# A two-layer decoder trunk on one Trainium2 core: one chunk of expert weights is brought into partitions 0 to 63 alone

## The chip, the cores and the metric

The kernel runs on one core of one Trainium2 chip. The metric is the device time of one execution in microseconds (us). Three executions of the kernel before took 1298.48, 1296.72 and 1298.28 us: a median of 1298.28.

## The reference

Input is one sequence of 256 tokens of 1024 numbers, all in float32. Layer 0 is attention (eight block-sparse heads, eight indexer-sparse heads) and a dense SwiGLU of 2816. Layer 1 is multi-head latent attention and then the part that this case is about, a mixture of eight experts of which each token uses two:

```python
top_val, top_idx = lax.top_k(logits, TOP_K)          # 2 of 8
gates = jax.nn.softmax(top_val, axis=-1)
combine = jnp.sum(jax.nn.one_hot(top_idx, N_EXPERTS) * gates[..., None], axis=1)
y = jnp.zeros_like(ht)
for e in range(N_EXPERTS):
    y = y + combine[:, e:e + 1] * swiglu(ht, w_gate[e], w_up[e], w_down[e])
```

`w_gate_o` and `w_up_o` are 1024 x 3584 for each expert, `w_down_o` is 3584 x 1024. Every expert has some tokens, so all 24 matrices are read: 352 MB out of the 424 MB that the kernel moves.

## The kernel before, in words

The first 400 us are layer 0 and the attention of layer 1. They read their weights in chunks of up to 1 MB through a ring `raw`.

The experts are computed in four pairs (`PAIRS`), a "large" expert with up to 96 tokens (three tiles of 32) and a "small" one with up to 64 (two tiles of 32). Tokens beyond that go through spare rounds, which don't run on this input. The weights of a pair come in 48 chunks (`PAIR_CHUNKS`), each of 128 partitions x 3584 numbers, 14,336 bytes in each partition and 1792 KB in all. A pair has six phases of eight chunks: large gate, large up, small gate, small up, large down, small down (`PHASES`, L59). Chunk k of gate or up holds rows 128 (k % 8) to 128 (k % 8) + 127 of the matrix, one row in each partition.

The whole stage is a ring of eleven places (`RING`, L270; `E_PLACES`): chunk n goes to place n % 11 and raises that place's own semaphore by 16 when it has landed. SyncE (SP) issues one transfer for each chunk, in order (`expert_chunk`, L388). Before chunk n it waits until TensorE has finished chunk n - 11 (`mm_done`, L392). A down row of 1024 numbers does not divide 3584, so two down chunks are used together, and `before` says which one frees the place. The last chunk of all comes in two transfers (L401, L402). So the order of work is written out by hand: SP's program is one list of transfers, TensorE's is one list of products, and the two are tied by `mm_done` in one direction and by the landing semaphores in the other.

TensorE packs four products side by side in its columns: a tile of 32 tokens is the stationary operand for one quarter of the output columns, and four such quarters are accumulated at once. For one gate or up chunk of the small expert that is 2 tiles x 2 column pieces (512 and 384) x 4 quarters = 16 matmul instructions in the program, which the profile counts as 32 (`tile_products`, L2292). Between the chunks TensorE also turns picks and results (L2235, L2342), brings back results (L2244), and gathers the next pair's tokens (`gather`, L2221) into PSUM. From there ScalarE and VectorE copy them to `xe` (L812, L1564).

In the last pair, chunk k = 23 (`SG + 7`) is the eighth and last chunk of the small gate. It is number 167 of the 192 chunks. In `pair` TensorE reaches it just after `turn_picks`.

Of the kernel before, what the change touches and what calls it, by code (L numbers as in the profile page):

```python
# [18 lines left out]
P = 128  # L19
S = 256  # L20
TT = S // P
D = 1024
DC = D // P
# [26 lines left out]
NT = 512  # L50
# [7 lines left out]
HALF = P // 2  # L58
# [6 lines left out]
E_PLACES = 11  # L65
# [5 lines left out]
X_CAP = L_CAP + S_CAP  # L71
YC = D // 4
SPARES = NE + PAIRS

SPARE_DOWN = 4 * FE_TILES
SPARE_CHUNKS = SPARE_DOWN + FFE // P // 2
# [6 lines left out]
def hybrid_trunk(nc, x, rel_bias, mix_norm_e, w_in_e, moba_q_norm, moba_k_norm, dsa_q_norm,  # L83
# [30 lines left out]
    C_OUTO = plan([rows(w_out_o, kh * 512, 4, n * NT, NT) for n in range(2) for kh in range(2)])  # L114
    C_ROUTE = plan([rows(w_router, 0, DC, 0, NE)])
    C_MOE = len(chunks)

    with ExitStack() as ctx:
        sems = {}

        def sem(name):
            if name not in sems:
                sems[name] = ctx.enter_context(nc.semaphore(name))
            return sems[name]
# [108 lines left out]
        xT, z1 = place(z + 2 * EW, "xT", [P, DC, S])  # L233
        ffg, _ = place(z1, "ffg", [P, D])
        junk, _ = place(z2, "junk", [P, TT, NT])
        xe = nc.alloc_sbuf_tensor_at("xe", [P, DC, X_CAP], f32, offset=a_hi_at)
        back_l = nc.alloc_sbuf_tensor_at("back_l", [P, L_TILES, S], f32, offset=a_hi_at + 4 * DC * X_CAP)
        xpick = cst[:, K_MASK:K_MASK + TT * X_CAP].rearrange("p (t s) -> p t s", t=TT)
# [40 lines left out]
        def place_of(n):  # L279
            return RING[n % E_PLACES]  # L280

        def landed(n):
            return ex_full[n % E_PLACES], 16 * (n // E_PLACES + 1)

        def before(n):

            m = n - E_PLACES
            return m + 1 if m % PAIR_CHUNKS >= DOWN and m % 2 == 0 else m

        LAST = PAIRS * PAIR_CHUNKS - 1  # L290
        LAST_AT = NT + D

# [45 lines left out]

            return [u for u in range(FE_TILES) if done(u) + late + u % 2 == k]  # L340

        M_SPARE = C_MOE + PAIRS * PAIR_CHUNKS
        F_SPARE = [16 * len(range(i, C_MOE, RAW)) for i in range(RAW)]
        H_SPARE, L_SPARE = H_MOE, L_MOE
        SPARE_BACK = (6, 7, 4, 5)
# [24 lines left out]
        def _(sp):  # L370
            for c, src in enumerate(chunks):
# [10 lines left out]
                if c >= RAW:  # L382
# [2 lines left out]
                sp.dma_start(raw[:, c % RAW, 0:k * n].rearrange("p (k n) -> p k n", k=k), src)\  # L385
                    .then_inc(raw_full[c % RAW], 16)

            def expert_chunk(p, k, e):  # L388
                n = p * PAIR_CHUNKS + k
                at = k % 8  # L390
                if n >= E_PLACES:
                    sp.wait_ge(mm_done, C_MOE + before(n) + 1)  # L392
                if k >= DOWN:
                    rows_g = w_down_o[0][bass.ds(e, 1), at // 2 * QW:(at // 2 + 1) * QW, :]
                    src = rows_g.rearrange("a (p k) n -> p a (k n)", p=P)[:, :, at % 2 * EW:(at % 2 + 1) * EW]
                else:
# [77 lines left out]
        def _(act):  # L474
# [332 lines left out]
            def gathered(p):  # L807

                for i in (0, 2):
                    act.wait_ge(sem("moe_gath"), 3 * p + i + 1)  # L810
                    a, b = GATHERED[i]
                    nc.scalar.activation(xe[:, a:b, :], PS[:, GATHER[i], 0:(b - a) * X_CAP].rearrange("p (d t) -> p d t", d=b - a),  # L812
                                         ACT.Copy).then_inc(sem("x_act"), 1)

            def large_silu(p, j):

                act.wait_ge(mm_done, C_MOE + p * PAIR_CHUNKS + 8)
                nc.scalar.activation(e_l[:, j, :], two_banks(LARGE_GATE[j]), ACT.Silu).then_inc(sem("l_silu"), 1)

            def large_turned(p, j):  # L820
# [2 lines left out]

            def small_silu(p, j):

                act.wait_ge(mm_done, C_MOE + p * PAIR_CHUNKS + SU)
                nc.scalar.activation(e_s[:, j, :], two_banks(SMALL_GATE[j]), ACT.Silu).then_inc(sem("s_silu"), 1)

            def small_turned(p, j):
# [2 lines left out]

            def large_result(p):

                act.wait_ge(mm_done, C_MOE + p * PAIR_CHUNKS + SMALL_DOWNS)
                for j in range(L_TILES):
                    nc.scalar.activation(y_l[:, j, :], PS[:, LARGE_DOWN[j], 0:YC], ACT.Copy).then_inc(sem("l_y"), 1)

            def small_result(p):

                act.wait_ge(mm_done, C_MOE + (p + 1) * PAIR_CHUNKS)
                nc.scalar.activation(y_s[:, 0, :], PS[:, SMALL_DOWN[0], 0:YC], ACT.Copy).then_inc(sem("s_y0"), 1)

            def pair(p, follow):
# [78 lines left out]
        def _(dve):  # L923
# [655 lines left out]

            def large_mul(p, j):  # L1580
                dve.wait_ge(sem("l_silu"), 3 * p + j + 1)
                dve.wait_ge(mm_done, C_MOE + p * PAIR_CHUNKS + SG)
                nc.vector.tensor_tensor(e_l[:, j, :], two_banks(LARGE_UP[j]), e_l[:, j, :], ALU.mult).then_inc(sem("l_mul"), 1)  # L1583

            def small_mul(p, j):
                dve.wait_ge(sem("s_silu"), 2 * p + j + 1)
                dve.wait_ge(mm_done, C_MOE + p * PAIR_CHUNKS + DOWN)
                nc.vector.tensor_tensor(e_s[:, j, :], two_banks(SMALL_UP[j]), e_s[:, j, :], ALU.mult).then_inc(sem("s_mul"), 1)  # L1588

            def small_result(p):  # L1590
                dve.wait_ge(mm_done, C_MOE + (p + 1) * PAIR_CHUNKS)
                nc.vector.tensor_copy(y_s[:, 1, :], PS[:, SMALL_DOWN[1], 0:YC]).then_inc(sem("s_y1"), 1)

            def pair(p, follow):
# [136 lines left out]
        def _(pe):  # L1731
# [489 lines left out]
            def gather(p):  # L2221

                pe.wait_ge(sem("moe_pick"), p + 2)
                for i, (a, b) in enumerate(GATHERED):
                    for dc in range(a, b):
                        for t in range(TT):
                            ins = nc.tensor.matmul(PS[:, GATHER[i], (dc - a) * X_CAP:(dc - a + 1) * X_CAP],  # L2227
                                                   xn[:, t, dc * P:(dc + 1) * P], xpick[:, t, :], start=t == 0, stop=t == 1)
                    ins.then_inc(sem("moe_gath"), 1)

            def turn_picks(p):
# [63 lines left out]
            def tile_products(p, k, j):  # L2295

                small, kind = PHASES[k // 8]
                at = k % 8
                w = place_of(p * PAIR_CHUNKS + k)
                tile_waits(p, k, j)  # L2300
                x0 = (L_CAP if small else 0) + j * Q
                bank = {"g": (LARGE_GATE, SMALL_GATE), "u": (LARGE_UP, SMALL_UP)}[kind][small][j]
                for c0, c in ((0, NT), (NT, QW - NT)):
                    for g in range(4):
                        ins = nc.tensor.matmul(PS[g * Q:(g + 1) * Q, bank + c0 // NT, 0:c], xe[:, at, x0:x0 + Q],  # L2305
                                               w[:, g * QW + c0:g * QW + c0 + c], start=at == 0, stop=at == DC - 1)
                return ins

            def gate_up(p, k):
                pe.wait_ge(*landed(p * PAIR_CHUNKS + k))  # L2310
                for j in range(S_TILES if PHASES[k // 8][0] else L_TILES):
                    ins = tile_products(p, k, j)
                ins.then_inc(mm_done, 1)
# [7 lines left out]
            def down(p, k):  # L2321
                small, _ = PHASES[k // 8]
                G, half = k % 8 // 2, k % 2
                n = p * PAIR_CHUNKS + k
# [12 lines left out]
                ins.then_inc(mm_done, 1)  # L2337
# [206 lines left out]
```

## Time and profile before

| | us |
|---|---|
| median of three executions | 1298.28 |
| the profiled execution, its own time | 1298.05 |
| its span, first to last instruction | 1296.2 |
| TensorE busy | 1243.5 (96%) |
| VectorE, ScalarE, GpSimd busy | 339.2, 286.8, 39.3 |
| moved by DMA | 423.64 MB, 327 GB/s over the span |

The span is the time from the first to the last instruction of the program. The own time is 1.85 us longer. A busy TensorE in this profile is not TensorE at its peak, since the ends of its pipelined matmuls are modelled. The 16 DMA engines have one row in the profile: their mean busy share. Packets are counted by queue. `hardware_dynamic` queue q1 is SP's own, `instruction` queue q8 brings blocks of instructions.

### The profile page before, as it was taken

The numbers are of one execution on the slowest core, as the hardware profiler recorded it, in microseconds if no ns is written. First come the engines' busy times: TensorE is split into PE (matmuls) and PEld (weight loads), VectorE is DVE, ScalarE is ACT, GpSimd is POOL, SyncE is SP. The second block draws the span as 40 slices with busy tenths as digits, with TensorE's granted clock in tenths as the row PEclk, the third lists the DMA queues.
The fourth block names the chain that finished last, engine by engine and source line by source line (L and its number), as shares of the span: only waits on it lengthen the run. The fifth ranks groups of instructions, "written<-read, shape, count | busy, mean of one in ns | idle before, by whom it ended". The sixth has DMA issues, their size and how long they took to land.

```text
span 1296.2 us, 27225 instructions
## 1 busy us (share of the span) xinstructions
PE 1243.5 (96%) x12500; PEld 718.2 (55%) x12501; DVE 339.2 (26%) x701; ACT 286.8 (22%) x499; POOL 39.3 (3%) x48
## 2 busy tenths in 40 slices
PE   7998999999999999999999999999998999998896
PEld 6865788888756774344653344663342664333364
DVE  5877565445347550010010020010010000001001
ACT  5575562425237621010000000000000000000000
POOL 1012000000002200000000000000000000000000
PEclk9999999999998999999999999999999999999999
DMA  9632455365353389999999999999999999999994
GB/s 351 229 130 81 147 188 181 118 228 165 88 192 122 145 361 419 409 418 426 424 425 425 425 426 426 425 424 425 426 426 426 425 425 423 427 425 425 427 422 172
DMA packets 64108, 423.64 MB, mean 327 GB/s; under 512 B 5760, under 2 KB 13686, under 8 KB 39414
## 3 DMA queue, kind: packets, MB, share of 16 engines
q1 hardware_dynamic: 62780, 419.09, 80.0%
q0 software_dynamic: 992, 2.69, 0.7%
q8 instruction: 99, 1.62, 0.5%
q14 instruction: 19, 0.16, 0.0%
q10 hardware_dynamic: 218, 0.08, 0.0%
HBM read 420.77 MB, written 1.07 MB: 325 GB/s over the span
## 4 chain that ended last, share of the span: by engine, by line
PE 82%; DMA 10%; DVE 4%; ACT 3%; issue 1%; SPq 0%; DVEq 0%; ACTq 0%
PE PS L2305 33%; PE PS L2334 16%; PE PS L1733 7%; PE PS L1734 7%; PE PS L1737 7%; DMA places_raw<-in_w_down_o_dram 6%; DMA places<-in_w_down_o_dram 3%; PE PS L2068 2%; PE PS L2342 2%; PE PS L2244 1%; DVE w_r L947 1%; PE PS L2227 1%; PE PS L1857 1%; ACT w_r L487 1%; PE PS L2080 1%
## 5 line engine op out<-in xcount | busy, mean ns | idle before, releaser
L2305 PE MATMUL PS<-places_raw,xe 128*32 128x512 f32 (+1 forms) x3760 | 362.3, 540 | 10.2 <-DMA places_raw<-in_w_up_o_dram 10.1
L2305 PEld LDWEIGHTS PS<-places_raw,xe 128*32 128x32 f32 x3760 | 119.4, 110 | 240.1 <-issue 219.3
L1733 PE MATMUL PS<-w_r,a_hi 128*128 128x512 f32 (+4 forms) x400 | 148.2, 374 | 5.3 <-DVE a_lo L976 4.4
L1734 PE MATMUL PS<-w_r,a_lo 128*128 128x512 f32 (+4 forms) x400 | 145.6, 368 | 0.0
L947 DVE TENSOR_TENSOR w_r<-raw,w_r 128x2048 fp32r<-128x2048 f32 (+4 forms) x61 | 128.9, 2144 | 44.0 <-ACT w_r L487 43.9
L2305 PE MATMUL PS<-places,xe 128*32 128x512 f32 (+1 forms) x1360 | 133.3, 540 | 4.0 <-DMA places<-in_w_up_o_dram 4.0
L487 ACT ACTIVATE w_r<-raw 128x2048 fp32r<-128x2048 f32 (+4 forms) x61 | 106.5, 1801 | 14.9 <-PE PS L1737 13.1
L2334 PE MATMUL PS<-places_raw,e_l 128*32 128x256 f32 x1848 | 106.4, 380 | 2.1 <-DMA places_raw<-in_w_down_o_dram 2.1
L1737 PE MATMUL PS<-w_r,a_hi 128*128 128x512 f32 (+4 forms) x400 | 103.2, 365 | 0.3 <-DVE w_r L947 0.3
L2305 PEld LDWEIGHTS PS<-places,xe 128*32 128x32 f32 x1360 | 43.2, 110 | 87.8 <-issue 80.3
L1733 PEld LDWEIGHTS PS<-w_r,a_hi 128*128 128x128 f32 x400 | 76.3, 191 | 19.6 <-issue 7.0
L1583 DVE TENSOR_TENSOR e_l<-PS,e_l 128x896 f32<-128x896 f32 x12 | 12.3, 1086 | 278.7 <-PE PS L2305 278.7
L2334 PEld LDWEIGHTS PS<-places_raw,e_l 128*32 128x32 f32 x1848 | 60.7, 110 | 42.6 <-DMA places_raw<-in_w_down_o_dram 3.5
L1734 PEld LDWEIGHTS PS<-w_r,a_lo 128*128 128x128 f32 x400 | 76.5, 191 | 11.0
L1737 PEld LDWEIGHTS PS<-w_r,a_hi 128*128 128x128 f32 x400 | 72.7, 190 | 13.0 <-DVE w_r L947 1.7
L2334 PE MATMUL PS<-places_raw,e_s 128*32 128x256 f32 x1288 | 73.9, 379 | 0.8 <-DMA places<-in_w_down_o_dram 0.8
L1571 DVE TENSOR_TENSOR X<-X,PS 128x512 f32<-128x512 f32 x32 | 19.9, 683 | 171.5 <-PE PS L2244 171.5
L2334 PEld LDWEIGHTS PS<-places_raw,e_s 128*32 128x32 f32 x1288 | 42.5, 110 | 29.0 <-DMA places<-in_w_down_o_dram 1.3
L2334 PE MATMUL PS<-places,e_l 128*32 128x256 f32 x840 | 51.1, 379 | 0.0
L822 ACT ACTIVATE e_l<-PS 128x896 f32<-128x896 f32 x12 | 11.0, 917 | 176.8 <-PE PS L2342 176.8
L831 ACT ACTIVATE e_s<-PS 128x896 f32<-128x896 f32 x8 | 7.3, 918 | 150.5 <-PE PS L2342 150.5
L1588 DVE TENSOR_TENSOR e_s<-PS,e_s 128x896 f32<-128x896 f32 x8 | 8.4, 1086 | 117.1 <-PE PS L2305 117.1
(328 smaller groups left out, 1029.4 us busy)
## 6 DMA issues: line engine op xcount, KB each, us to landing
places_raw<-in_w_gate_o_dram SPq DMA_DIRECT2D x48, 1792.0 KB, 26.5
places_raw<-in_w_up_o_dram SPq DMA_DIRECT2D x46, 1792.0 KB, 31.1
places_raw<-in_w_down_o_dram SPq DMA_DIRECT2D x44, 1792.0 KB, 37.0
places<-in_w_down_o_dram SPq DMA_DIRECT2D x19, 1792.0 KB, 36.3
places<-in_w_up_o_dram SPq DMA_DIRECT2D x18, 1792.0 KB, 31.6
places<-in_w_gate_o_dram SPq DMA_DIRECT2D x16, 1792.0 KB, 30.2
raw<-in_w_in_e_dram SPq DMA_DIRECT2D x12, 1024.0 KB, 10.3
raw<-in_w_down_e_dram SPq DMA_DIRECT2D x11, 1024.0 KB, 5.0
```

Source lines behind the costliest of these rows:

```text
L487: nc.scalar.activation(w_r[:, hi_slot(c), 0:n], raw[:, c % RAW, 0:n], ACT.Copy).then_inc(hi_done, 1)
L947: nc.vector.tensor_tensor(w_r[:, c % RAW, 0:n], raw[:, c % RAW, 0:n], w_r[:, hi_slot(c), 0:n], ALU.subtract).then_inc(lo_done, 1)
L1571: nc.vector.tensor_tensor(X[:, :, cols], X[:, :, cols], PS[:, bank, :].rearrange("p (t n) -> p t n", t=TT), ALU.add)\
L1733: nc.tensor.matmul(dst, xh, wh, start=first, stop=False)
L1734: nc.tensor.matmul(dst, xl, wh, start=False, stop=False)
L1737: return nc.tensor.matmul(dst, xh, wl, start=False, stop=last)
L1857: nc.tensor.matmul(dst, v_of(h, 0), probs_t[:, h % 2, 0:S], start=True, stop=False)
L2068: ins = nc.tensor.matmul(PS[:, bank + t, 0:n], latT[:, x0 + k, t * P:(t + 1) * P], w[:, k, :], start=k == 0, stop=k == kn - 1)
L2080: ins = nc.tensor.transpose(PS[0:QKD, turn_group_bank(h), s * S + t * P:s * S + (t + 1) * P], qk[:, g % 2, (s * TT + t) * GH + h % GH, :], ...
L2305: ins = nc.tensor.matmul(PS[g * Q:(g + 1) * Q, bank + c0 // NT, 0:c], xe[:, at, x0:x0 + Q], w[:, g * QW + c0:g * QW + c0 + c], start=at == ...
L2334: ins = nc.tensor.matmul(PS[g * Q:(g + 1) * Q, bank, 0:YC], acts[:, j, kk * P + G * Q:kk * P + (G + 1) * Q], down_columns(n - half, kk, g) ...
L2342: ins = nc.tensor.transpose(PS[:, bank + kk // 4, kk % 4 * P:(kk % 4 + 1) * P], e[:, j, :].rearrange("p (r k) -> p k r", k=QB)[:, kk, :], ...
```

## The change

The ring now has 193 numbers. Chunk k = 23 of the last pair takes two of them, 167 and 168, and everything behind it moves up by one (`number`). Its 128 rows go into partitions 0 to 63 of two places, 64 rows each. Each half is brought by eight transfers of eight rows: transfer i fills partitions i, i + 8, ..., i + 56. The landing count of that place rises by 8 x 16.

TensorE multiplies each half over 64 partitions. The second half of the rows needs its tokens in partitions 0 to 63 too, so `gather` makes that piece once more (two small matmuls), and ScalarE copies it to a tile of its own, `xeb`.

```diff
+HALVED = SG + 7
+ENGINES_LOW = 8
...
+    def number(p, k):
+        return p * PAIR_CHUNKS + k + (p == PAIRS - 1 and k > HALVED)
+
+    FIRST_HALF = number(PAIRS - 1, HALVED)
+    PLACED = [(p, k) for p in range(PAIRS) for k in range(PAIR_CHUNKS)]
+    PLACED.insert(FIRST_HALF, PLACED[FIRST_HALF])
...
         def landed(n):
-            return ex_full[n % E_PLACES], 16 * (n // E_PLACES + 1)
+            return ex_full[n % E_PLACES], sum(16 * (ENGINES_LOW if m in (FIRST_HALF, FIRST_HALF + 1) else 1)
+                                              for m in range(n % E_PLACES, n + 1, E_PLACES))
...
+            def half_chunk(n, at, e):
+
+                sp.wait_ge(mm_done, C_MOE + before(n) + 1)
+                r0 = at * P + (n - FIRST_HALF) * HALF
+                src = w_gate_o[0][bass.ds(e, 1), r0:r0 + HALF, :].rearrange("a (j i) n -> i j a n", i=ENGINES_LOW)
+                dst = place_of(n)[0:HALF].rearrange("p (a n) -> p a n", a=1)
+                for i in range(ENGINES_LOW):
+                    sp.dma_start(dst[i:HALF:ENGINES_LOW], src[i]).then_inc(landed(n)[0], 16)
+
             def expert_chunk(p, k, e):
-                n = p * PAIR_CHUNKS + k
+                n = number(p, k)
                 at = k % 8
+                if n == FIRST_HALF:
+                    half_chunk(n, at, e)
+                    half_chunk(n + 1, at, e)
+                    return
...
+                    if p == PAIRS - 1 and i == 2:
+                        nc.scalar.activation(xeb[0:HALF, :], PS[0:HALF, GATHER[i], 2 * X_CAP:2 * X_CAP + S_CAP], ACT.Copy)\
+                            .then_inc(sem("xeb_set"), 1)
...
+                    if p == PAIRS - 1 and i == 2:
+                        for t in range(TT):
+                            ins = nc.tensor.matmul(PS[0:HALF, GATHER[i], 2 * X_CAP:2 * X_CAP + S_CAP],
+                                                   xn[:, t, DC * P - HALF:DC * P], xpick[:, t, L_CAP:X_CAP], start=t == 0, stop=t == 1)
...
+            def half_products(n, k):
+
+                at = k % 8
+                for u in range(2):
+                    if u:
+                        pe.wait_ge(*landed(n + 1))
+                        pe.wait_ge(sem("xeb_set"), 1)
+                    w = place_of(n + u)
+                    for j in range(S_TILES):
+                        x0 = L_CAP + j * Q
+                        xs = xeb[0:HALF, j * Q:(j + 1) * Q] if u else xe[0:HALF, at, x0:x0 + Q]
+                        for c0, c in ((0, NT), (NT, QW - NT)):
+                            for g in range(4):
+                                ins = nc.tensor.matmul(PS[g * Q:(g + 1) * Q, SMALL_GATE[j] + c0 // NT, 0:c], xs,
+                                                       w[0:HALF, g * QW + c0:g * QW + c0 + c], start=False, stop=u == 1)
+                    ins.then_inc(mm_done, 1)
```

The remaining edits only put `number(p, k)` where `p * PAIR_CHUNKS + k` stood.

## Rows read from the trace of the kernel before

**Rows 1.** The page, part 3: DMA queues over the whole span.
```profile
q1 hardware_dynamic: 62780, 419.09, 80.0%
q8 instruction: 99, 1.62, 0.5%
```

**Rows 2.** Stretches: us; PE, PEld, DVE, ACT, POOL busy; granted clock; DMA share, GB/s.
```profile
560.00:600.00 40.00, 40.00 (x420) 14.69 (x415) 2.55 (x7) 3.47 (x4) 0.00 (x0) 1.00 1.01 426
1100.00:1140.00 40.00, 40.00 (x428) 13.69 (x424) 0.00 (x0) 2.54 (x3) 0.00 (x0) 1.00 1.01 425
1178.00:1217.00 39.00, 29.90 (x298) 9.25 (x296) 1.88 (x4) 1.73 (x2) 0.00 (x0) 1.00 1.01 427
1262.00:1266.00 4.00, 4.00 (x76) 2.89 (x71) 0.61 (x2) 0.00 (x0) 0.00 (x0) 1.00 1.00 418
```

**Rows 3.** Timeline of TensorE: start, us, line, shapes, count, idle before and releaser.
```profile
1171.57 6.22 PE L2305 MATMUL PS<-places_raw,xe 128*32 128x512 f32 x64
1177.72 1.31 PE L2235 MATMUL PS<-cst,gpick 128*128 128x128 f32 x10
1178.97 3.21 PE L2305 MATMUL PS<-places,xe 128*32 128x512 f32 x32
1182.98 3.21 PE L2305 MATMUL PS<-places,xe 128*32 128x512 f32 x32 [0.80 <-DMA places<-in_w_up_o_dram]
1187.26 3.21 PE L2305 MATMUL PS<-places_raw,xe 128*32 128x512 f32 x32 [1.06 <-DMA places_raw<-in_w_up_o_dram]
1191.55 3.21 PE L2305 MATMUL PS<-places_raw,xe 128*32 128x512 f32 x32 [1.08 <-DMA places_raw<-in_w_up_o_dram]
...
1217.67 4.09 PE L2334 MATMUL PS<-places_raw,e_l 128*32 128x256 f32 x72 [1.07 <-DMA places_raw<-in_w_down_o_dram]
...
1274.94 0.41 PE L2334 MATMUL PS<-places_raw,e_s 128*32 128x256 f32 x2 [0.80 <-DMA places<-in_w_down_o_dram]
...
1279.22 3.00 PE L2334 MATMUL PS<-places,e_s 128*32 128x256 f32 x50 [0.62 <-DMA places<-in_w_down_o_dram]
...
1286.12 2.01 PE L2244 MATMUL PS<-y_s,back_s 32*128 32x256 f32 x32 [0.64 <-DVE y_s L1592]
```

**Rows 4.** The same view of stretches at the end of the stream.
```profile
1266.00:1268.00 2.00, 2.00 (x44) 1.23 (x40) 1.88 (x4) 0.00 (x0) 0.00 (x0) 1.00 0.80 336
1268.00:1270.00 2.00, 2.00 (x44) 1.22 (x40) 0.00 (x0) 0.00 (x0) 0.00 (x0) 1.00 0.60 248
1270.00:1274.00 4.00, 4.00 (x80) 2.21 (x68) 0.00 (x0) 0.00 (x0) 0.00 (x0) 1.00 0.50 208
1274.00:1278.00 4.00, 3.20 (x62) 1.85 (x62) 0.00 (x0) 0.00 (x0) 0.00 (x0) 1.00 0.48 198
1278.00:1282.00 4.00, 3.38 (x64) 1.85 (x60) 0.00 (x0) 0.00 (x0) 0.00 (x0) 1.00 0.44 185
1282.00:1286.00 4.00, 3.48 (x68) 1.73 (x56) 0.42 (x1) 0.38 (x1) 0.00 (x0) 1.00 0.03 12
```

**Rows 5.** DMA queues from 465 to 1282 us.
```profile
q8 instruction: 79, 1.29, 0.6%
```

**Rows 6.** DMA queues from 1178 to 1282 us.
```profile
q8 instruction: 11, 0.18, 0.7%
```

**Rows 7.** SP's timeline: issues around the chunk, and at the program's start.
```profile
1137.74 0.33 SPq L404 DMA_DIRECT2D places<-in_w_gate_o_dram  x1
1142.12 0.33 SPq L404 DMA_DIRECT2D places<-in_w_up_o_dram  x1
1146.63 21.88 SPq L404 DMA_DIRECT2D places_raw<-in_w_up_o_dram  x6
...
4.71 8.43 SPq L385 DMA_DIRECT2D raw<-in_w_in_e_dram  x5
```

**Rows 8.** Issues from 1130 to 1150 us: count, KB, median us to landing.
```profile
places<-in_w_gate_o_dram SPq DMA_DIRECT2D x1, 1792.0 KB, 40.9
```

**Rows 9.** Line L402, the last transfer of all.
```profile
DMA to landing us min/median/max: 35.3/35.3/35.3
```

**Rows 10.** Timeline around the last gather, all engines.
```profile
1032.81 4.61 PE L2227 MATMUL PS<-cst,xn 128*128 128x160 f32 x32
1037.46 0.44 ACT L812 ACTIVATE xe<-PS 128x320 f32<-128x320 f32 x1 [2.15 <-PE PS L2227]
```

More of the change, by code:

```diff
@@ L235, in hybrid_trunk @@
         junk, _ = place(z2, "junk", [P, TT, NT])
+        xeb, _ = place(z2, "xeb", [P, S_CAP])
         xe = nc.alloc_sbuf_tensor_at("xe", [P, DC, X_CAP], f32, offset=a_hi_at)
@@ L282, in landed @@
         def landed(n):
-            return ex_full[n % E_PLACES], 16 * (n // E_PLACES + 1)
+            return ex_full[n % E_PLACES], sum(16 * (ENGINES_LOW if m in (FIRST_HALF, FIRST_HALF + 1) else 1)
+                                              for m in range(n % E_PLACES, n + 1, E_PLACES))
         def before(n):
             m = n - E_PLACES
-            return m + 1 if m % PAIR_CHUNKS >= DOWN and m % 2 == 0 else m
-        LAST = PAIRS * PAIR_CHUNKS - 1
+            _, k = PLACED[m]
+            return m + 1 if k >= DOWN and k % 2 == 0 else m
+        LAST = number(PAIRS - 1, PAIR_CHUNKS - 1)
         LAST_AT = NT + D
@@ L340, in units @@
             return [u for u in range(FE_TILES) if done(u) + late + u % 2 == k]
-        M_SPARE = C_MOE + PAIRS * PAIR_CHUNKS
+        M_SPARE = C_MOE + LAST + 1
         F_SPARE = [16 * len(range(i, C_MOE, RAW)) for i in range(RAW)]
@@ L815, in large_silu @@
             def large_silu(p, j):
-                act.wait_ge(mm_done, C_MOE + p * PAIR_CHUNKS + 8)
+                act.wait_ge(mm_done, C_MOE + number(p, 8))
                 nc.scalar.activation(e_l[:, j, :], two_banks(LARGE_GATE[j]), ACT.Silu).then_inc(sem("l_silu"), 1)
@@ L824, in small_silu @@
             def small_silu(p, j):
-                act.wait_ge(mm_done, C_MOE + p * PAIR_CHUNKS + SU)
+                act.wait_ge(mm_done, C_MOE + number(p, SU))
                 nc.scalar.activation(e_s[:, j, :], two_banks(SMALL_GATE[j]), ACT.Silu).then_inc(sem("s_silu"), 1)
@@ L833, in large_result @@
             def large_result(p):
-                act.wait_ge(mm_done, C_MOE + p * PAIR_CHUNKS + SMALL_DOWNS)
+                act.wait_ge(mm_done, C_MOE + number(p, SMALL_DOWNS))
                 for j in range(L_TILES):
@@ L839, in small_result @@
             def small_result(p):
-                act.wait_ge(mm_done, C_MOE + (p + 1) * PAIR_CHUNKS)
+                act.wait_ge(mm_done, C_MOE + number(p, PAIR_CHUNKS))
                 nc.scalar.activation(y_s[:, 0, :], PS[:, SMALL_DOWN[0], 0:YC], ACT.Copy).then_inc(sem("s_y0"), 1)
@@ L1581, in large_mul @@
                 dve.wait_ge(sem("l_silu"), 3 * p + j + 1)
-                dve.wait_ge(mm_done, C_MOE + p * PAIR_CHUNKS + SG)
+                dve.wait_ge(mm_done, C_MOE + number(p, SG))
                 nc.vector.tensor_tensor(e_l[:, j, :], two_banks(LARGE_UP[j]), e_l[:, j, :], ALU.mult).then_inc(sem("l_mul"), 1)
@@ L1586, in small_mul @@
                 dve.wait_ge(sem("s_silu"), 2 * p + j + 1)
-                dve.wait_ge(mm_done, C_MOE + p * PAIR_CHUNKS + DOWN)
+                dve.wait_ge(mm_done, C_MOE + number(p, DOWN))
                 nc.vector.tensor_tensor(e_s[:, j, :], two_banks(SMALL_UP[j]), e_s[:, j, :], ALU.mult).then_inc(sem("s_mul"), 1)
             def small_result(p):
-                dve.wait_ge(mm_done, C_MOE + (p + 1) * PAIR_CHUNKS)
+                dve.wait_ge(mm_done, C_MOE + number(p, PAIR_CHUNKS))
                 nc.vector.tensor_copy(y_s[:, 1, :], PS[:, SMALL_DOWN[1], 0:YC]).then_inc(sem("s_y1"), 1)
@@ L2298, in tile_products @@
                 at = k % 8
-                w = place_of(p * PAIR_CHUNKS + k)
+                w = place_of(number(p, k))
                 tile_waits(p, k, j)
@@ L2307, in tile_products @@
                 return ins
-            def gate_up(p, k):
-                pe.wait_ge(*landed(p * PAIR_CHUNKS + k))
+            def half_products(n, k):
[13 more added lines that the diff above has]
+                    ins.then_inc(mm_done, 1)
+            def gate_up(p, k):
+                n = number(p, k)
+                pe.wait_ge(*landed(n))
+                if n == FIRST_HALF:
+                    half_products(n, k)
+                    return
                 for j in range(S_TILES if PHASES[k // 8][0] else L_TILES):
@@ L2323, in down @@
                 G, half = k % 8 // 2, k % 2
-                n = p * PAIR_CHUNKS + k
+                n = number(p, k)
                 pe.wait_ge(*landed(n))
```

## The prediction

> **What bounds the kernel now.** I read the page's queues first, then stretches of the expert stage, then TensorE's timeline for who waits, then the same stretches at the very end.
>
> In the expert stage the DMA share is 1.01 at 425 to 427 GB/s at 560, 1100 and 1178 us, and still 1.00 at 1262 us [rows 2]. A chunk of 1792 KB is 1.835 MB, so at 427 GB/s it takes 4.30 us. TensorE shows the same beat once it has caught up: its starts on the small up chunks are 1182.98, 1187.26 and 1191.55, 4.29 apart, with 3.21 of work and a wait for a DMA of about 1.07 in each [rows 3]. So the stream of weights is the bound, and TensorE keeps just within it. Before 1178 us it is fully busy (40.00 of 40.00) [rows 2]. It then waits at nine chunks, from 1182.98 to 1217.67, and those nine are 0.80, 1.06, 1.08 and six more of about the same, some 9.7 us in all. From 1217.67 TensorE works without a DMA wait in the down phases, until 1274.94 and 1279.22, where it waits 0.80 and 0.62 again [rows 3]. The last bytes and TensorE arrive together.
>
> The end of the stream is the part to look at. The share does not fall from 1.00 to 0. It is 0.80, 0.60, then 0.50 with 208 GB/s, 0.48 and 0.44, and 0.03 after 1282 [rows 4]. The GB/s halve with it. A steady 0.50 is eight of sixteen DMA engines at full pace and eight with nothing left to do. When does each half end? The early half's excess over 0.50 is 2.0 x 0.30 + 2.0 x 0.10 = 0.8 us of share from 1266 on, and its full share is 0.50, so on average it ends at 1266 + 1.6 = 1267.6. The late half has 4.0 x 0.44 + 4.0 x 0.03 = 1.88 us of share from 1278 on, so it ends at 1278 + 3.8 = 1281.8. **Half of the DMA engines is 14 us, more than three chunks, behind the other half.** Every chunk spans all engines, so TensorE always waits for the late half.
>
> Where do the 14 us come from? Queue q8 brings instruction blocks, 99 of them with 1.62 MB, 16 KB each, and 0.5% of sixteen engines' span: 0.005 x 16 x 1296 / 99 = 1.05 us each [rows 1]. From 465 to 1282 us there are 79 [rows 5]. Over eight engines that is 79 x 1.05 / 8 = 10.4 us, over sixteen it would be 5.2 and even. I infer that they go through one half of the engines only. From 1178 us on there are eleven [rows 6], or 1.4 us of lead, so at the changed chunk the lead is already about 14.2 - 1.4 = 12.8 us.
>
> **The change, part by part.**
>
> *The transfers.* If the eight-row transfers run on eight engines, and these are the early eight, then the late half skips one chunk and is 4.29 us earlier at every later one. The early half carries that chunk alone: 16 rows for each engine in place of 8, so 4.29 us more, out of a lead of 12.8. It stays 12.8 - 4.29 - 4.29 = 4.2 us ahead, and never ends a wait. Its end goes from 1267.6 to 1271.9, the late half's from 1281.8 to 1277.5. Gain in the stream: 4.29.
>
> No row of before shows a transfer of eight rows, so its pace has bounds. The lower one is the full pace of eight engines, 208 GB/s [rows 4], 8.8 us for the chunk. The upper one is half of that, if two engines have to share a way into the memory, some 17.5 us; this is my second case below. I take the lower, since all rows of eight busy engines are at it.
>
> *TensorE.* The chunk is multiplied as two halves of 32 counted matmuls each. A shorter contraction saves nothing: 32 rows deep and 256 wide take 2.01 / 32 = 0.063 us, 128 deep and 256 wide 3.00 / 50 = 0.060 [rows 3]. So it costs 3.21 more. Its start at 1178.97 comes behind `turn_picks`, and does not move. The next chunk starts at 1178.97 + 6.42 = 1185.4 instead of 1182.98. From there each chunk takes 3.21 against a landing every 4.29. To be 4.29 ahead of today by 1217.67, TensorE must swallow 3.21 + 4.29 = 7.5 us of waits, and 9.7 are there. It has them after about seven chunks, so the down phases begin 4.29 earlier. They are TensorE's own work, and move as one piece. The waits at 1274.94 and 1279.22 move with the late half, and the tail behind them (back products, additions, stores) is unchanged. Cost at the end: 0. Without these waits it would be 3.2.
>
> *The extra gather and copy.* 4 of the counted matmuls at 4.61 / 32 = 0.14, 0.6 us, and a copy below 0.44 [rows 10], both at 1037 us, where 140 us of full TensorE follow but the stream is the bound. PE's 3.21 + 0.6 = 3.8 still fit: 3.8 + 4.3 = 8.1 of 9.7. The first product that needs `xeb` comes 140 us later, and `back_large` waits for `xe` some 20 us later. Cost 0.
>
> *SP.* Sixteen issues in place of one. At 0.33 each they are 5.3 us, at 8.43 / 5 = 1.69, the pace of the program's first issues, 27 us [rows 7]. The next issue was at 1142.12, 4.4 us after 1137.74. The second half takes the place that the next chunk had, so the eleven issues behind it each wait for one TensorE chunk more, about 4 us. Against this stands the queue: issue to landing is 40.9 us here [rows 8], and still 35.3 at the last transfer [rows 9]. Less the lead, the early half has 28 us queued. 5.3 - 4.4 + 4 = 5 us later is hidden. At 27 us it would just be used up, so I keep that end for the range. The six issues at 1146.63 take 21.88 us, which is 3.6 each, so SP stands at a full queue there and makes up for lost time.
>
> *Instructions.* 36 matmuls and 36 loads more, where 25,001 stand in 99 blocks or 253 each: 0.28 of a block, at 1.05 on one late engine, up to 1.05 if it falls ahead of the last chunk. I take 0.3.
>
> Sum from the profiled execution's own time: 1298.05 - 4.29 + 0.3 = 1294.06. The median of the runs shown is 0.23 above that execution, so I say 1294.1, between the two.
>
> **Two rules of the Trainium skill.** Which half is early stands in no row. By "DMA: Bandwidth & Descriptors", the section on why a DMA increments its semaphore by 16, a transfer issued from SP runs on the largest number up to 16 that divides its outermost dimension, on the lowest-numbered engines. By its section on the descriptor swizzle, engines 0 to 7 serve partitions 0 to 63. An outermost dimension of 8 would then confine these transfers to engines 0 to 7, and a 64-row transfer would not be confined. No run here shows either yet. "SBUF — State Buffer", the section on door 1, speaks against the change: four neighbouring partitions and the four 32 above them share one port, and a port carries 27.2 GB/s, about what one engine moves. That is the rule behind my second case, which gives the sum 1297.4.
>
> **The rivals.**
>
 Then the 16 rows take 17.16 us where the 8 took 4.29, and the early half is 12.9 later: it ends at 1267.6 + 12.9 = 1280.5 on average, its last engine (0.60 still at 1268 to 1270 [rows 4]) at about 1282. The end was 1281.8. So 0 to 1.3 us of the gain stay, I say 0.65: 1298.05 - 0.65 = 1297.4. For it: the steady full pace needs every engine apart. Against it: eight busy engines reach 208 GB/s, and engines a row or two apart need not meet. The point from which it decides is an extra of 8.5 us on the early half.
>
> *C, the early half is the other one.* Then the late half, which every chunk waits for, carries the chunk alone: 4.29 more at once, from 1182.98 on, and nothing in the down phases gives it back. 1298.05 + 4.29 = 1302.3. With B's half pace on top it would be 1310.9. For it: no row names the engines. Against it: instruction blocks have to be on one half or the other, and I have no row for which.
>
> *D, the transfers are not confined.* Eight-row transfers over all sixteen engines leave the halves as they are. TensorE's 3.8 us go into the 9.7 of waits: 1298.05 + 0.3 = 1298.3.
>
> *E, the queue runs dry.* SP's sixteen issues near 1.7 us each and the place that is one chunk short hold later transfers back: 27 - 28 + 4 = 3 us of stall against 4.29 of gain, or the same without the gain. 1297 to 1301.
>
> **How the numbers follow.** A 0.44, B 0.33, C 0.13, D 0.05, E 0.05. The forecast is A's, 1294.1. What a measurement of this kernel can tell from no change is about 0.2%, 2.6 us. A is faster by more than that. B, D and part of E are within it. C and the rest of E are slower. Faster 0.44, same 0.38, slower 0.18. The range goes from 1293.2 (A with the whole 4.29 and the 0.6 that TensorE would still wait) over B and D to 1299.3, and leaves out C and E's slow part.
>
> **What would show it.** In A the share at the end falls from 1.00 straight to below 0.5 within some 6 us instead of 14. TensorE has two runs of 3.21 at 1179, no DMA wait for about seven chunks behind them, then waits of 1.07 again, and starts the down phases near 1213.4. In B the landing of the second half comes near or after 1182, TensorE waits for it or for the next chunk, and the down phases start near 1217. In C they start at 1222 or later, and the half-share tail grows beyond 14 us. In D the tail stays 14 us long. SP's issues at 1138 show which of 0.33 and 1.7 us holds. The prediction is wrong if the down phases don't start within 1 us of 1213.4.

## The result, and the profile after

The changed kernel takes 1316.53 us (median of four executions, 1313.84 to 1318.12) against 1298.38 before (four executions). The ratio is 1.0147, 95% interval 1.0132 to 1.0162: 18 us slower. The forecast was 1294.1 with a range up to 1299.3. The profiled execution took 1317.39, its span is 1315.6.

TensorE's timeline answers to [rows 3] (start, us, line, shapes, count, idle before and its releaser; L2337 is the line of the whole products, L2354 of the halves):

```profile
1164.46 3.21 PE L2337 MATMUL PS<-places_raw,xe 128*32 128x512 f32 x32
1171.26 3.21 PE L2337 MATMUL PS<-places,xe 128*32 128x512 f32 x32 [3.59 <-DMA places<-in_w_gate_o_dram]
...
1179.46 4.89 PE L2337 MATMUL PS<-places_raw,xe 128*32 128x512 f32 x32 [3.05 <-DMA places_raw<-in_w_gate_o_dram]
1185.36 3.21 PE L2337 MATMUL PS<-places_raw,xe 128*32 128x512 f32 x32 [1.00 <-DMA places_raw<-in_w_gate_o_dram]
...
1190.35 3.21 PE L2354 MATMUL PS<-places,xe 64*32 64x512 f32 x32 [0.54 <-DMA places<-in_w_gate_o_dram]
1197.44 6.20 PE L2354 MATMUL PS<-places,xeb 64*32 64x512 f32 x32 [3.88 <-DMA places<-in_w_gate_o_dram]
1203.57 14.01 PE L2337 MATMUL PS<-places_raw,xe 128*32 128x512 f32 x128
...
1233.23 4.91 PE L2337 MATMUL PS<-places_raw,xe 128*32 128x512 f32 x32 [2.78 <-DMA places_raw<-in_w_up_o_dram]
1237.95 4.07 PE L2387 MATMUL PS<-places_raw,e_l 128*32 128x256 f32 x72
```

The waits begin ahead of the halves, at 1171, for gate chunks that were issued before them. The first half starts at 1190.35 where the whole chunk had started at 1178.97, and the down phases begin at 1237.95 instead of 1217.67. That is 20.3 us later. 1.0 of it stood already at 1164.46, where the same chunk had started at 1163.48, so 19.3 came in the stretch from 1165 to 1238.

Behind the waits of 3.05 and 3.88 us TensorE's granted clock is lower: down to 0.50 from 1200 to 1205, which is the lower of its two levels (1.2 GHz), and the 32 matmuls of the second half take 6.20 us in place of 3.21. This cost nothing at the end. At 1218.65 TensorE waits for a transfer again (1.07, and 1.01 at 1298.87), so it had caught up with the stream.

The stretches of the changed kernel, with the columns of [rows 2], show what was late:

```profile
1150.00:1155.00 5.00, 5.00 (x51) 2.14 (x47) 2.81 (x3) 0.35 (x1) 0.00 (x0) 1.00 1.02 433
1160.00:1165.00 5.00, 5.00 (x50) 2.25 (x53) 0.00 (x0) 1.35 (x2) 0.00 (x0) 1.00 1.03 198
1165.00:1170.00 5.00, 2.67 (x32) 0.69 (x24) 0.00 (x0) 0.48 (x1) 0.00 (x0) 1.00 0.98 272
1170.00:1175.00 5.00, 3.74 (x44) 1.51 (x48) 0.00 (x0) 0.00 (x0) 0.00 (x0) 1.00 1.01 201
1175.00:1180.00 5.00, 1.95 (x32) 1.17 (x28) 2.48 (x4) 0.00 (x0) 0.00 (x0) 0.95 1.01 233
1180.00:1185.00 5.00, 4.36 (x32) 1.01 (x24) 0.00 (x0) 0.00 (x0) 0.00 (x0) 0.71 1.03 310
1185.00:1190.00 5.00, 4.46 (x42) 2.01 (x42) 0.15 (x1) 0.00 (x0) 0.00 (x0) 1.00 0.99 275
1190.00:1195.00 5.00, 3.21 (x32) 0.92 (x32) 1.47 (x3) 0.00 (x0) 0.00 (x0) 1.00 1.00 235
1200.00:1205.00 5.00, 5.00 (x30) 0.97 (x24) 0.00 (x0) 1.29 (x2) 0.00 (x0) 0.50 1.02 433
```

The DMA share stays at 1.0 while the GB/s fall towards a half: every engine is busy, and the packets take longer. The trace keeps the time of each packet. A row of 14,336 bytes took 0.54 us in the median before; from 1160 to 1165 us the fastest of 69 took 1.01, and the medians of the seven stretches from 1160 to 1195 are 0.66 to 1.11. The seven stretches from 1160 to 1195 average 246 GB/s, so 35 x (1 - 246 / 425) = 14.7 us of stream are lost, for all sixteen engines together.

And at the end, with the columns of [rows 4]:

```profile
1286.00:1290.00 4.00, 4.00 (x80) 2.44 (x76) 2.13 (x4) 0.00 (x0) 0.00 (x0) 1.00 0.64 262
1290.00:1294.00 4.00, 4.00 (x80) 2.38 (x76) 0.00 (x0) 0.00 (x0) 0.00 (x0) 1.00 0.23 95
1294.00:1298.00 4.00, 3.86 (x72) 2.08 (x64) 0.00 (x0) 0.00 (x0) 0.00 (x0) 1.00 0.13 47
1298.00:1302.00 4.00, 3.13 (x60) 1.93 (x64) 0.00 (x0) 0.00 (x0) 0.00 (x0) 1.00 0.12 47
```

The half-share step of [rows 4] is gone. In its place stands a step at 0.12 to 0.13, which is two engines of sixteen, and these two end the stream alone. The trace also keeps the time of each landing update, which is the step by which one DMA engine raises the semaphore of a place when its part of a transfer has landed. They tell the same: for each row of the first half one update arrives, 48 of them from 1160.1 to 1171.5 us and 16 from 1181.4 to 1190.3, and for the second half 48 from 1168.6 to 1181.3 and 16 from 1189.9 to 1197.4. Six engines had done their rows by 1181.3, two did theirs behind that.

The last landing update of the whole stream came at 1281.1 us before and at 1300.7 in the changed kernel, 19.6 later, and the two profiled executions differ by 19.3. In twelve of the thirteen traces the time from that update to the end of the execution is 16.7 to 17.1 us (18.25 in the run with neighbouring partitions). So the end of the stream decides the time.

So there are two questions: why the whole stream ran at little more than half pace (246 of 425 GB/s) for 35 us, and which engines are the last two.

### The profile page after: what moved, and what is told of

Same layout as the page of the kernel before. It is cut to its first block, busy times and chain, and to the rows that moved or that the text cites. A ratio compares the mean times of both kernels' runs of the same rounds, so it can differ in the third digit from the quotient of the medians.

```text
span 1315.6 us, 27344 instructions
## 1 busy us (share of the span) xinstructions
PE 1255.1 (95%) x12536; PEld 721.6 (55%) x12537; DVE 338.8 (26%) x701; ACT 287.0 (22%) x500; POOL 39.3 (3%) x48
## 3 DMA queue, kind: packets, MB, share of 16 engines
HBM read 420.77 MB, written 1.07 MB: 321 GB/s over the span
## 4 chain that ended last, share of the span: by engine, by line
PE 78%; DMA 14%; DVE 4%; ACT 3%; issue 1%; another core or an unknown queue 0%; SPq 0%; DVEq 0%; ACTq 0%
PE PS L2337 30%; PE PS L2387 16%; PE PS L1761 7%; PE PS L1765 7%; PE PS L1762 7%; DMA places_raw<-in_w_down_o_dram 6%; DMA places_raw<-in_w_gate_o_dram 4%; DMA places_raw<-in_w_up_o_dram 4%; PE PS L2096 2%; PE PS L2395 1%; PE PS L2276 1%; DVE w_r L975 1%; PE PS L2255 1%; PE PS L1885 1%; ACT w_r L512 1%
## 5 line engine op out<-in xcount | busy, mean ns | idle before, releaser
L2337 PE MATMUL PS<-places_raw,xe 128*32 128x512 f32 (+1 forms) x3792 | 370.1, 545 | 10.6 <-DMA places_raw<-in_w_up_o_dram 6.6
L2337 PEld LDWEIGHTS PS<-places_raw,xe 128*32 128x32 f32 x3792 | 121.5, 111 | 246.5 <-issue 226.7
L2337 PE MATMUL PS<-places,xe 128*32 128x512 f32 (+1 forms) x1296 | 128.5, 545 | 8.5 <-DMA places<-in_w_up_o_dram 4.9
L2337 PEld LDWEIGHTS PS<-places,xe 128*32 128x32 f32 x1296 | 41.6, 111 | 89.8 <-issue 78.0
L1761 PEld LDWEIGHTS PS<-w_r,a_hi 128*128 128x128 f32 x400 | 76.1, 190 | 19.6 <-issue 7.1
```

The costliest lines, as they stand in the source:

```text
L1761: nc.tensor.matmul(dst, xh, wh, start=first, stop=False)
```

## The experiments

Eleven runs were made, of ten kernels (the aligned one ran twice). Where no count is given, the time is of one execution. Three theories stood for the slow stretch: W, partitions (several engines write into one group of four partitions); R, the source's pitch, which is the distance in memory between the rows that one transfer reads; S, a semaphore update behind each row.

**Aligned partitions.** The halves as in the change, but transfer i fills every fourth partition:

```diff
-                src = ....rearrange("a (j i) n -> i j a n", i=ENGINES_LOW)
+                src = ....rearrange("a (h j i) n -> h i j a n", h=2, i=4)
...
-                    sp.dma_start(dst[i:HALF:ENGINES_LOW], src[i]).then_inc(landed(n)[0], 16)
+                    h0 = 32 * (i // 4)
+                    sp.dma_start(dst[h0 + i % 4:h0 + 32:4], src[i // 4, i % 4]).then_inc(landed(n)[0], 16)
```

> The changed kernel took 1317, and its DMA stream fell to some 250 GB/s from 1158 to 1196 us at a full busy share. Here the same sixteen eight-row transfers take other partitions: transfer i fills i % 4 + 32 (i // 4) and every fourth one behind it, so that eight engines write eight different groups of four partitions, as they do in a 128-row transfer. Theory W (several engines in one group of partitions hold each other up, and all others with them): no slow stretch, all packets near 0.54 us, time 1302.6 if some of the eight engines are of the late half (4.3 above before), 1294 if none is. Theory R (the source pitch of eight rows, 112 KB, is bad for the memory; it is 56 KB here): also fast, or half as slow. Theory S (a semaphore update behind each single row stalls an engine): still near 1316, since there are as many transfers and updates.

Measured: 1300.87 in one execution, beside 1297.17. The same kernel was then run twelve times:

> The aligned eight-row transfers once more, to measure them: two late engines carry sixteen rows. Theory: 4.29 us above before, 1301 to 1303. Rival (late engines don't carry it, the one look at 1300.9 was scatter): at or below before.

Measured: 1300.97 over twelve executions (1299.15 to 1302.86), ratio 1.0026, interval 1.0017 to 1.0035, that is 2.2 to 4.5 us above before. The stream in the same stretches:

```profile
1160.00:1165.00 5.00, 5.00 (x51) 2.14 (x47) 0.00 (x0) 0.92 (x1) 0.00 (x0) 1.00 1.01 427
1170.00:1175.00 5.00, 5.00 (x64) 1.95 (x60) 2.48 (x4) 0.00 (x0) 0.00 (x0) 1.00 0.99 422
1190.00:1195.00 5.00, 3.92 (x44) 1.20 (x40) 0.00 (x0) 0.00 (x0) 0.00 (x0) 1.00 1.01 427
...
1270.00:1274.00 4.00, 4.00 (x80) 2.44 (x76) 1.69 (x3) 0.00 (x0) 0.00 (x0) 1.00 0.61 251
1274.00:1278.00 4.00, 4.00 (x81) 2.37 (x77) 0.00 (x0) 0.00 (x0) 0.00 (x0) 1.00 0.29 121
1278.00:1282.00 4.00, 3.42 (x64) 1.82 (x56) 0.00 (x0) 0.00 (x0) 0.00 (x0) 1.00 0.12 49
1282.00:1286.00 4.00, 3.27 (x62) 1.98 (x65) 0.00 (x0) 0.00 (x0) 0.00 (x0) 1.00 0.11 43
```

The slow stretch is gone with the same number of transfers, rows and updates: S falls. Between the medians of the changed and the aligned kernel lie 15.6 us, or 15.0 when each is set against the kernel before in its own comparison. The source's pitch changed too, from 112 KB to 56. The next two kernels show that it is not the cause, so these 15 us come from which partitions a transfer fills. The step of two engines stays, and with it some 3 us above before: the last landing update comes at 1284.6, 3.5 later than before.

**The source's pitch alone.** Two kernels read eight neighbouring rows, so their result for this chunk is another. One writes every eighth partition, as the change does, the other every fourth:

```diff
-                src = ....rearrange("a (j i) n -> i j a n", i=ENGINES_LOW)
+                src = ....rearrange("a (i j) n -> i j a n", i=ENGINES_LOW)      # every eighth partition
...
+                src = ....rearrange("a (h i j) n -> h i j a n", h=2, i=4)       # every fourth partition
```

> The partitions of each transfer are as in the changed kernel (i, i + 8, ...), but the eight rows read are neighbours in memory (pitch 14 KB), so that rows of this one chunk meet other tokens' numbers than they should and the result of this chunk is another. Theory W: still 1316, with the same slow stretch. Theory R: no slow stretch, 1294 to 1303. Theory S: still 1316.

Measured: 1320.26.

> The partitions of the run with every fourth partition, but the eight rows read are neighbours in memory (pitch 14 KB in place of 56 KB), so rows of this chunk meet other tokens' numbers. Theory W (partitions decide): as that run, no slow stretch, 1300 to 1302. Theory R (source pitch decides; 14 KB and 112 KB were both slow): a slow stretch again, 1315 to 1320.

Measured: 1299.67. At one and the same pitch of 14 KB the partitions decide between 1320 and 1300, a difference far above the scatter of one kernel's executions (4.3 us from lowest to highest in the changed one). R falls.

**More engines in one group.** Eight neighbouring rows into eight neighbouring partitions, and one 64-row transfer for each half:

```diff
-                    sp.dma_start(dst[i:HALF:ENGINES_LOW], src[i]).then_inc(landed(n)[0], 16)
+                    sp.dma_start(dst[i * ENGINES_LOW:(i + 1) * ENGINES_LOW], src[i]).then_inc(landed(n)[0], 16)    # neighbours, and the source as above
...
+                sp.dma_start(dst, src).then_inc(landed(n)[0], 16)    # the other kernel: one transfer of 64 rows, no loop, one count of 16
```

> Eight-row transfers into eight neighbouring partitions each, 8 i to 8 i + 7, from eight neighbouring rows. Theory W: four engines now share a group of four partitions where it was two, so the sixteen rows cost four times their share, and the slow stretch is about twice as long and deep: 1330 to 1340. Theory R: fast, 1294 to 1303. Theory S: 1316.

Measured: 1315.68. It is as slow as the change, and no slower.

> Each half comes in one transfer of 64 rows, over all engines if the number of rows decides; the places, the products and the extra gather stay. Theory W: two engines share each group of four partitions, so the chunk costs 8.6 us of stream in place of 4.3: 1302.7. Theory R and S: no slow stretch, the stream as before, 1298.4 with TensorE's 3.8 us inside its waits.

Measured: 1307.54, beside 1297.17: slow, as W says, but by 10.4 us where I had 4.3. Its stream:

```profile
1160.00:1165.00 5.00, 4.06 (x39) 1.66 (x38) 0.00 (x0) 0.92 (x1) 0.00 (x0) 1.00 1.02 221
1170.00:1175.00 5.00, 5.00 (x61) 2.23 (x56) 0.84 (x2) 0.00 (x0) 0.00 (x0) 0.87 0.91 370
1180.00:1185.00 5.00, 5.00 (x54) 2.23 (x50) 0.87 (x2) 0.00 (x0) 0.00 (x0) 1.00 1.00 209
```

It is slow twice. The landing updates of its two halves come from 1162.1 to 1171.1 us for eight engines and from 1179.1 to 1188.3 for the other eight. Early and late engines reach these rows at different times, and each time the whole stream is slow. So W holds in its direction, and my sizes for it were wrong both ways. The loss does not follow the number of engines in a group.

**Half and half.** First half aligned, second half with the change's stride. Against the aligned kernel (`wide` is the source as the change has it):

```diff
+                    if n > FIRST_HALF:
+                        sp.dma_start(dst[i:HALF:ENGINES_LOW], wide[i]).then_inc(landed(n)[0], 16)
+                        continue
```

> First half of the chunk aligned, second half with the changed kernel's stride of eight partitions. If the loss goes with the number of rows that meet in groups: half of the 16 us between aligned and changed, so about 1309. If one such stretch is enough to throw the engines out of step: 1315 or more. If it takes both: near 1301.

Measured: 1310.71. Of the 15.6 us between aligned and changed, 64 of the 128 rows bring 9.7. The loss grows with the rows. Whether it does so in proportion (7.8) one execution can't tell, since the aligned kernel's executions alone span 3.7 us.

**The upper partitions.** The aligned transfers, moved to partitions 64 to 127, and multiplied from there. The first half meets other tokens' numbers in it:

```diff
-                dst = place_of(n)[0:HALF].rearrange("p (a n) -> p a n", a=1)
+                dst = place_of(n)[HALF:P].rearrange("p (a n) -> p a n", a=1)
...
+                        xs = xe[HALF:P, at, x0:x0 + Q]
```

> As the run with every fourth partition, but in partitions 64 to 127, multiplied from there with the tokens that lie there, so that the first half meets other tokens' numbers. If the number of rows alone picks the engines (the first eight), they now write groups of partitions that the other eight write in all other transfers: a slow stretch, over 1308. If the partitions pick them, the other eight carry it, no slow stretch, and the time tells how many of those are late: 1301 to 1303 if any is, 1294 if none.

Measured: 1317.45. The same rows at the same stride took 1300.97 in partitions 0 to 63, so the upper ones cost 16.5 us more. The landing updates show which engines carry them: again 48 of the first half come early (1159.0 to 1170.1 us) and 16 late (1180.9 to 1189.2). So six early engines and two late ones are at work, as in partitions 0 to 63. By the tiny transfers below, the other eight engines are two early ones and six late ones and would have given 16 and 48. The number of rows picks the engines, and the partitions don't change them.

This trace also has the plainest picture of the loss. From 1182 to 1190 us only the two late engines are still at these rows, and yet all 112 rows that start in that time take 1.14 to 1.16 us where they took 0.54 in the median before, at a DMA share of 1.01 and 201 GB/s. 112 x 1.15 / 8 is 16, so all sixteen engines are busy at about half their pace.

**Which engines are late.** Tiny transfers behind chunk 167 of the kernel before, one of each kind from one row to eight:

```diff
+                if n == PROBE_AT:
+                    sp.dma_start(probe[0:1, 0:8], consts[0:1, 0:8]).then_inc(sem('probe1'), 16)
+                    sp.dma_start(probe[0:2, 8:16], consts[0:2, 0:8]).then_inc(sem('probe2'), 16)
...
```

> The kernel before, with eight tiny transfers (32 bytes in each of 1, 2, ... 8 partitions, each with a line and a semaphore of its own) issued right behind chunk 167. Each lands when the queues of the engines that carry it have drained to it, so its landing tells whether the last of its engines is early or late. If rows decide the engines and all of the first eight are early: all eight land about 12 us before chunk 167 does (1166 against 1179). If two of the first eight are late, as the changed kernel's landings look: the transfers up to some number of rows land at about 1166, and from there on at 1175 to 1179. Time 1298, since eight issues of 0.6 us are hidden.

Measured: 1295.12, in one execution. The landing updates of these transfers, one for each engine of a transfer, in us (each semaphore also gets one update at its issue, left out here):

```
rows   landings of the engines
1      1162.44
2      1162.62 1163.57
3      1162.82 1162.88 1163.75
4      1163.01 1163.06 1163.94 1164.13
5      1163.20 1163.25 1164.12 1164.33 1165.35
6      1163.40 1163.43 1164.30 1164.52 1165.55 1174.59
7      1163.58 1163.61 1164.48 1164.71 1165.74 1174.80 1175.39
8      1162.38 1163.76 1163.78 1164.65 1164.90 1165.94 1175.00 1175.59
chunk 167: eight from 1162.17 to 1165.16, eight from 1174.00 to 1176.14
```

The same two clusters stand in chunk 167 itself, eight engines early and eight late. The gap between them is 8.8 us, and their means lie 11.6 apart. Each further row adds one engine: the first five are early, the sixth and the seventh late, the eighth early. So a transfer of eight rows takes six early engines and two late ones. That fits the 48 and 16 updates of the changed kernel, and these are the two of the 0.12 step.

**The mechanism that the forecast had assumed.** Aligned five-row transfers, for early engines alone. Against the aligned kernel:

```diff
+EARLY = 5
-                    sp.dma_start(dst[h0 + i % 4:h0 + 32:4], src[i // 4, i % 4]).then_inc(landed(n)[0], 16)
+                    sp.dma_start(dst[h0 + i % 4:h0 + 4 * EARLY:4], src[i // 4, i % 4, 0:EARLY]).then_inc(landed(n)[0], 16)
```

> The tiny transfers showed that of the first eight engines the first five and the eighth are early, the sixth and seventh late. Here the aligned transfers have five rows each, for the first five engines alone: sixteen rows for each of them, 80 rows in all. The other 48 rows of this chunk are left out (their partitions hold older weights). This is what the forecast had assumed: all late engines skip the chunk, early ones carry sixteen rows. Theory (late engines end the stream, 4.29 us a chunk): 1293 to 1294.5, some 4 us under before. Rival (the stream is one rate for all, or TensorE's double products bind): within 1 us of before.

Measured: 1291.94 over six executions (1290.52 to 1295.23), ratio 0.9958, interval 0.9945 to 0.9972: 3.6 to 7.1 us faster than before. It leaves out 48 rows, so it is no version to use, but the late engines skip the chunk in it and five early ones carry sixteen rows, as I had assumed. All its 80 landing updates have come by 1168.96 us. The missing rows alone do not explain the gain: if the stream had one rate for all engines, 48 of 128 rows would be worth 48 / 128 x 4.29 = 1.6 us, below the interval. TensorE:

```profile
1176.16 3.21 PE L2356 MATMUL PS<-places,xe 64*32 64x512 f32 x32
1179.19 3.19 PE L2356 MATMUL PS<-places,xeb 64*32 64x512 f32 x32
1182.31 18.34 PE L2339 MATMUL PS<-places_raw,xe 128*32 128x512 f32 x192
1201.72 3.21 PE L2339 MATMUL PS<-places,xe 128*32 128x512 f32 x32 [1.07 <-DMA places<-in_w_up_o_dram]
1206.02 3.21 PE L2339 MATMUL PS<-places_raw,xe 128*32 128x512 f32 x32 [1.08 <-DMA places_raw<-in_w_up_o_dram]
1210.32 4.09 PE L2389 MATMUL PS<-places_raw,e_l 128*32 128x256 f32 x72 [1.08 <-DMA places_raw<-in_w_down_o_dram]
```

Six chunks without a wait, then waits of 1.07 again. From the chunk's start to the down phases it takes 1210.32 - 1176.16 = 34.16 us. In the kernel before it was 1217.67 - 1178.97 = 38.70 [rows 3]. That is 4.54 less, where the forecast had 4.29.

**TensorE's part alone.** The kernel before, with the chunk's products made twice over partitions 0 to 63, so that half of its rows is left out:

```diff
+                if p == PAIRS - 1 and k == SG + 7:
+                    for u in range(2):
+                        part = slice(0, HALF)
...
```

> The kernel before with its own transfers and places; TensorE alone does the chunk's products twice with 64 partitions (0 to 63 both times, so half of the chunk's rows is left out and the other counted twice). 3.2 us more of work on TensorE just ahead of nine waits of 9.7 us in all. Theory: hidden, 1298.4, ratio within 0.1% of 1. Rival: 3.2 us on the path, 1301.6, ratio 1.0025.

Measured: 1296.77 over ten executions beside 1297.17, ratio 0.9992, interval 0.998 to 1.0003. The 3.2 us are hidden:

```profile
1177.92 6.22 PE L2319 MATMUL PS<-places,xe 64*32 64x512 f32 x64
1184.07 3.21 PE L2305 MATMUL PS<-places,xe 128*32 128x512 f32 x32
1187.10 3.19 PE L2305 MATMUL PS<-places_raw,xe 128*32 128x512 f32 x32
1190.69 3.21 PE L2305 MATMUL PS<-places_raw,xe 128*32 128x512 f32 x32 [0.40 <-DMA places_raw<-in_w_up_o_dram]
1195.00 3.21 PE L2305 MATMUL PS<-places_raw,xe 128*32 128x512 f32 x32 [1.09 <-DMA places_raw<-in_w_up_o_dram]
```

The waits of the next two chunks are gone, the third is down to 0.40, and from there on it is the kernel before.

## Why the prediction was wrong, step by step

**What bounds the kernel: right.** The late half of the engines ends the stream, and one chunk less for it is worth its 4.29 us. The five-row kernel shows it: 3.6 to 7.1 us, and 4.54 by the timeline. The lead itself is right too: in the trace of the kernel before, the mean landing update of the eight late engines comes 14.1 us behind that of the eight early ones at the last chunks, for the 14.2 that I read from [rows 4].

That instruction blocks make the lead was an inference, and the landing updates bear it out, though no run here took the blocks away. They show the lead growing through the whole stream, from 1.1 us at 550 to 12.2 at 1168. Over six chunks it grows by 0.27 to 0.58 us where two blocks of q8 start in that time (most often 0.39), by 0.57 to 0.59 with three, and by 0.45 to 0.80 with four. That is some 0.19 us a block for the mean of eight engines, or 8 x 0.19 = 1.5 us for the one engine that carries it (an estimate from these numbers). I had 1.05, the time of its packet. At the end one block shows by itself. In the changed kernel it starts at 1230.97, the last landing of the chunk then under way comes 6.0 us behind the one before in place of 4.3, and TensorE waits 2.78 at 1233.23 in place of 1.08. The aligned kernel has the same, with a block at 1214.82 and a wait of 2.77.

**The transfers, "if these are the early eight": wrong.** They are six early ones and two late ones. I had drawn two cases, all early and all late. One late engine among the eight is enough for the second, since each chunk waits for its last engine. That was case C with 1302.3, and the aligned kernel, where this error stands alone, measured 1300.97: 2.2 to 4.5 above before, for 4.29. The half-share step told how many engines are early. It could not tell which, and I gave C 0.13 only. One more step failed in C as I wrote it: I let the whole late half carry the chunk, and two engines of it were enough.

**The transfers, the pace: wrong, and the main loss.** I took "the lower, since all rows of eight busy engines are at it". But all those rows were of engines that write 128-row transfers. The upper bound was too small as well. Case B put the half pace on the eight engines that share, 8.6 us more on the early half, most of it inside its lead. What happened is a pace near half on all sixteen, 246 GB/s on average from 1160 to 1195 us, also after 1181.3, when only the two late engines were still at their rows (235 to 310 GB/s). An engine's lead is no cover against that. Aligned to changed is 1300.97 to 1316.53, so this term, which I had put at nothing, is 15.6 us. B's bound and C's 4.29 together gave 1310.9 in the text. This stood outside the range, and should have been inside: the two have different causes and can come together.

**TensorE, 3.21 us more within 9.7 us of waits: right.** 1296.77 with it alone. A half of 64 partitions takes 3.21 us like a whole chunk, as I had said.

**SP's sixteen issues: right, they are hidden.** They took 12.90 us, 0.8 each, within the bounds of 0.33 and 1.69. In the aligned kernel they took 15.17 us, and its stream stayed at 419 to 431 GB/s.

**Instructions, 0.3: too small to be seen.** Eleven blocks came from 1178 to 1282 us in the aligned kernel, as in [rows 6].

The sum with measured terms, one of which (14.7) is an estimate from the stretches: 1298.4, + 3.1 for two late engines with sixteen rows each (1300.97 - 1297.83, the kernel before in that comparison), + 14.7 for the stream at 246 GB/s, + 0 for TensorE and SP, is 1316.2, for 1316.53 measured.

The Trainium skill, "DMA: Bandwidth & Descriptors", in its section on why a DMA increments its semaphore by 16, has the number of rows choose the number of engines. The tiny transfers (one more update for each row) and the run in partitions 64 to 127 (48 and 16 updates again) agree. The Trainium skill, "SBUF — State Buffer", door 1, lets the pace go by the number of ports that are reached. The runs agree that sharing a group costs, and differ on the size: all sixteen engines paid, not those alone that shared. And the run in partitions 64 to 127 reaches as many groups as the aligned one, and still took 1317.45 against 1300.97, so the count of ports alone does not give the loss.

No version here that brings all 128 rows beats the kernel before. For the gain, all 128 rows must go through engines that are early, with one group of partitions to each. Five engines fill 40 partitions, so the chunk would need four places and four rounds of products, 3 x 3.21 = 9.6 us more on TensorE where 9.7 us of waits stand, before any gain. This is an estimate, since I did not build it.

## What to carry to other kernels

A DMA share that ends in a long step below 1.0 shows unequal queues, and here the height of the step counted the engines that were still at work (0.50 eight, 0.12 two). Before rows are moved to "the idle ones", find out which these are, with tiny transfers of one, two, three rows behind a large one. And keep each engine on the partitions that it has in a full 128-partition transfer: 128 rows outside that pattern cost 15 us here, on all engines. No trace here names the partitions of an engine in a full transfer. What the aligned runs show is a pattern for transfers of eight rows that left the stream at 419 to 431 GB/s: every fourth partition, with the first one at 0 to 3 or at 32 to 35.

## What was not expected of the hardware

- Two late engines writing out of their pattern held all sixteen engines well below full pace (235 to 310 GB/s from 1180 to 1195 us, and 201 in partitions 64 to 127) at a DMA share of 1.0. Why the others are hit stays open. No run separated a shared way into the memory from a blocked one. And in every slow kernel an engine both left its own group and met another engine there, so which of the two does it is not shown either.
- Four engines in one group (1315.68, one execution) cost no more than two (1316.53), and a plain transfer of 64 rows over all engines cost 10.4 us in place of 4.3.
- Late engines are a mixed set, two of the first eight and so six of the other eight, 9 to 14 us behind the rest. Why these, no row tells.
- An instruction block of 16 KB sets the engine that carries it back by some 1.5 us, an estimate from the growing lead. That is more than the 1.05 of its packet.
